# Second MLP product by seven half-size products in three of four quarters, weight sums on GpSimd, low parts by accumulating DMAs

## The reference, cut to what matters

```python
def squared_relu_mlp(h, w1, w2):
    return jnp.square(jax.nn.relu(h @ w1)) @ w2
...
        x = x + squared_relu_mlp(rms_norm(x, norm_mlp[i]), mlp_w1[i], mlp_w2[i])
```

## Time and profile before

| | |
|---|---|
| median of 3 runs | 2765.72 us (2764.86 to 2770.12) |
| the profiled execution: its time, its span | 2773.47 us, 2771.7 us |
| mean granted TensorE clock | 0.993 |
| busy share: TensorE, ScalarE, VectorE, GpSimd | 98%, 39%, 38%, 49% |
| matmuls of the MLP (L2009) | 6,144 |

### The profile page before, as it was taken

How to read it: one execution, slowest core, us unless ns; L and a number is a source line. 1 busy time by engine, 2 the same in 40 slices (tenths; PEclk the granted TensorE clock), 3 DMA queues, 4 the chain that set the end, 5 groups by cost and what they waited for, 6 DMA issues and landing times.

```text
span 2771.7 us, 37296 instructions
## 1 busy us (share of the span) xinstructions
PE 2716.1 (98%) x14594; PEld 2193.4 (79%) x14594; DVE 1046.8 (38%) x1966; ACT 1086.8 (39%) x1649; POOL 1359.7 (49%) x1042
## 2 busy tenths in 40 slices
PE   8999999999999999999899999999999999999999
PEld 6977688888766788888788887888888977688887
DVE  4044622113486512213777874311123044622112
ACT  5355633223446423324334344322234355533222
POOL 4577354445455354445444442445455576345443
PEclk9999999999999999999899999999999999999999
DMA  4322122323422123223312110232323322122232
GB/s 143 99 69 63 52 92 91 106 91 92 106 46 77 61 92 106 91 91 110 80 33 57 37 62 24 92 98 91 106 91 99 100 54 69 56 97 91 92 105 76
DMA packets 273439, 227.87 MB, mean 82 GB/s; under 512 B 29220, under 2 KB 260388, under 8 KB 273300
## 3 DMA queue, kind: packets, MB, share of 16 engines
q1 hardware_dynamic: 262578, 216.66, 25.9%
q10 hardware_dynamic: 10722, 9.28, 1.5%
HBM read 223.62 MB, written 2.30 MB: 82 GB/s over the span
## 4 chain that ended last, share of the span: by engine, by line
PE 91%; DVE 3%; ACT 2%; POOL 2%; issue 1%; DMA 1%; ACTq 0%; SPq 0%; DVEq 0%; POOLq 0%
PE bank L2009 50%; PE bank L1916 20%; PE bank L2132 4%; PE bank L2372 2%; PE bank L2512 2%; PE bank L2092 1%; PE bank L2189 1%; PE bank L2205 1%; POOL w_lo L620 1%; PE bank L1962 1%; PE bank L2169 1%; PE bank L2162 1%; PE bank L2219 1%; POOL arena L693 1%; PE bank L1943 1%
## 5 line engine op out<-in xcount | busy, mean ns | idle before, releaser
L620 POOL TENSOR_TENSOR w_lo<-raw,w_hi 128x512 fp32r<-128x512 f32 x808 | 1081.0, 1368 | 1087.0 <-ACT w_hi L777 1067.7
L777 ACT ACTIVATE w_hi<-raw 128x2048 fp32r<-128x2048 f32 x201 | 383.7, 1909 | 462.1 <-PE bank L2009 423.3
L2009 PE MATMUL bank<-h_hi,w_hi 128*128 128x512 f32 x1024 | 400.8, 391 | 0.0
L2009 PE MATMUL bank<-g_hi,w_hi 128*128 128x512 f32 x1024 | 398.6, 389 | 0.0
L2009 PE MATMUL bank<-h_hi,w_lo 128*128 128x512 f32 x1024 | 398.4, 389 | 0.0
L2009 PE MATMUL bank<-g_hi,w_lo 128*128 128x512 f32 x1024 | 398.4, 389 | 0.0
L2009 PE MATMUL bank<-h_lo,w_hi 128*128 128x512 f32 x1024 | 398.4, 389 | 0.0
L2009 PE MATMUL bank<-g_lo,w_hi 128*128 128x512 f32 x1024 | 398.4, 389 | 0.0
L1916 PE MATMUL bank<-h_hi,w_hi 128*128 128x512 f32 x776 | 317.3, 409 | 2.4 <-POOL w_lo L620 1.9
L1916 PE MATMUL bank<-h_lo,w_hi 128*128 128x512 f32 x776 | 310.5, 400 | 0.0
L1916 PE MATMUL bank<-h_hi,w_lo 128*128 128x512 f32 x776 | 307.8, 397 | 0.0
(11 more groups left out here) (276 smaller groups left out, 3805.0 us busy)
## 6 DMA issues: line engine op xcount, KB each, us to landing
raw<-in_mlp_w SPq DMA_DIRECT2D x128, 1024.0 KB, 5.4
raw<-in_a_w_in SPq DMA_DIRECT2D x48, 512.0 KB, 5.1
raw<-in_c_w_in SPq DMA_DIRECT2D x32, 512.0 KB, 5.5
raw<-in_a_w_in SPq DMA_DIRECT2D x12, 1024.0 KB, 5.2
raw<-in_b_w_in SPq DMA_DIRECT2D x18, 256.0 KB, 4.0
raw<-in_a_w_out SPq DMA_DIRECT2D x4, 1024.0 KB, 4.9
raw<-in_b_w_in SPq DMA_DIRECT2D x4, 1024.0 KB, 5.4
arena<-bias_scratch ACTq DMA_DIRECT2D x16, 256.0 KB, 3.6
```

The costliest lines, as they stand in the source:

```text
L620: ins = nc.gpsimd.tensor_tensor(w_lo[s][:, k, :], raw[s][:, k, :], w_hi[s][:, k, :].bitcast(F32), ALU.subtract)
L777: nc.scalar.activation(w_hi[s][:], raw[s][:], ACT.Copy).then_inc(w_hi_done, 1)
L2009: mm = nc.tensor.matmul(lin_bank[j][:], w[s][:, c, P * j:P * j + P], a[:, c, :], start=c + z == 0, stop=c == CT - 1 and z == 2)
```

## The change

In quarters 0 to 2 of each layer (`HALVED`) the second product of a chunk is made by a seven-product scheme (`down`): contraction tiles are taken in even and odd pairs, the chunk's two output tiles as two column tiles, the 512 tokens as two halves of 256. Of the chunk's weights three of four blocks are used as they are (`weight`), and four sums of blocks are formed (`weight_sum`); of the hidden activations four blocks and three sums (`hidden`, `hidden_sum`). Seven products of 4 contraction pairs x 3 matmuls of 256 columns go to parts of four PSUM banks, and VectorE adds them to or subtracts them from `x` in eight pieces of 128 x 256 (`add_part`). The fourth quarter keeps its form.

The weight sums are formed on GpSimd (`summed_weights`, four instructions of 128 x 512). Low parts of whole chunks and of the sums are formed otherwise than before: ScalarE writes the high part, then its negative into the low buffer, and a DMA issued by GpSimd adds the raw values to it (`add_raw`, and `add_sums` for the sums, which is written in the same way), two DMAs of 512 KB a chunk. The low parts of the three blocks used as they are come from VectorE (`weights_low`, 128 x 512). The sums of activations are formed by VectorE (`differences`, 128 x 256), rounded by ScalarE (128 x 768) and their low parts formed by VectorE. The loops over the quarters are written out on all engines. The diff, cut:

```diff
...
+        w_sum = [part(4 * TOK).rearrange("p (k q n) -> p k q n", k=4, q=4) for _ in range(2)]
...
+        ws_hi = [over_arena(f"ws_hi{s}", [P, 4, 4, P]) for s in range(2)]
+        ws_lo = [over_arena(f"ws_lo{s}", [P, 4, 4, P]) for s in range(2)]
+        gt_hi, gt_lo = over_arena("gt_hi", [P, 4, 3, HALF]), over_arena("gt_lo", [P, 4, 3, HALF])
...
+        def quads(m):
+            return m.rearrange("p (q z) (n c) -> p (z n) q c", z=2, n=2)
+        def half_banks(d):
+            return [bank[k][:, 0:HALF] for k in ((2, 3, 4, 5), (6, 7, 0, 1))[d % 2]]
...
+            def add_raw(n):
+                s = n % 2
+                for half in range(2):
+                    k = slice(4 * half, 4 * half + 4)
+                    pool.wait_ge(w_neg, 2 * split_no[n] + half + 1)
+                    pool.dma_start(w_lo[s][:, k, :].bitcast(F32), raw[s][:, k, :],
+                                   accum_op=ALU.add).then_inc(w_added[s][half], 16)
+            def summed_weights(n):
+                s, v = n % 2, 4 * half_no[n]
+                whole, sums = quads(raw[s][:]), w_sum[s]
+                pool.wait_ge(raw_loaded[s], raw_value[n])
...
+                nc.gpsimd.tensor_tensor(sums[:, 0], whole[:, 3], whole[:, 1], ALU.add).then_inc(ws_summed, 1)
+                pool.wait_ge(ws_summed, v + 1)
+                nc.gpsimd.tensor_tensor(sums[:, 1], sums[:, 0], whole[:, 0], ALU.add).then_inc(ws_summed, 1)
+                pool.wait_ge(ws_summed, v + 2)
+                nc.gpsimd.tensor_tensor(sums[:, 2], sums[:, 1], whole[:, 2], ALU.add).then_inc(ws_summed, 1)
+                nc.gpsimd.tensor_tensor(sums[:, 3], whole[:, 0], whole[:, 1], ALU.add).then_inc(ws_summed, 1)
...
+            def rounding(n):
+                if halved(n):
+                    sums_rounded(n)
+                    weights_rounded(n)
+                    return
                 s = n % 2
...
+                act.wait_ge(raw_loaded[s], raw_value[n])
+                if n >= 2:
+                    act.wait_ge(lin_done, tile0[n - 1])
+                if CHUNKS[n][0] != "mlp":
+                    nc.scalar.activation(w_hi[s][:], raw[s][:], ACT.Copy).then_inc(w_hi_done, 1)
+                    return
+                parts = [slice(4 * half, 4 * half + 4) for half in range(2)]
+                for k in parts:
+                    nc.scalar.activation(w_hi[s][:, k, :], raw[s][:, k, :], ACT.Copy).then_inc(w_high, 1)
+                for half, k in enumerate(parts):
+                    act.wait_ge(w_high, 2 * split_no[n] + half + 1)
+                    nc.scalar.activation(w_lo[s][:, k, :], w_hi[s][:, k, :].bitcast(F32), ACT.Copy,
+                                         scale=-1.0).then_inc(w_neg, 1)
+            def sums_rounded(n):
+                s, v = n % 2, half_no[n]
+                act.wait_ge(lin_done, tile0[n - 1])
+                for half in range(2):
+                    k = slice(2 * half, 2 * half + 2)
+                    act.wait_ge(ws_summed, 4 * v + 2 * half + 2)
+                    nc.scalar.activation(ws_hi[s][:, k], w_sum[s][:, k], ACT.Copy).then_inc(w_high, 1)
+                    act.wait_ge(w_high, 2 * split_no[n] + half + 1)
+                    nc.scalar.activation(ws_lo[s][:, k], ws_hi[s][:, k].bitcast(F32), ACT.Copy,
+                                         scale=-1.0).then_inc(w_neg, 1)
+                    if half == 0:
...
+                        nc.scalar.activation(quads(w_hi[s][:])[:, 0], quads(raw[s][:])[:, 0], ACT.Copy).then_inc(wp_high, 1)
+            def weights_rounded(n):
+                s = n % 2
+                nc.scalar.activation(quads(w_hi[s][:])[:, 2:4], quads(raw[s][:])[:, 2:4], ACT.Copy).then_inc(wp_high, 1)
...
+            def squares(li, q, p, z):
...
+                act.wait_ge(relu_done, g + 1)
+                if p or q:
+                    act.wait_ge(gt_done, 4 * u - 2) if z == 0 else act.wait_ge(gl_done, v - 1)
+                dst = pieces[:, 3:5, :] if z else pieces[:, 0:2, :][:, ::-1, :]
+                src = sq[z].rearrange("p (k n) -> p k n", k=2)
+                nc.scalar.activation(dst, src, ACT.Square).then_inc(gsq_done, 1)
+            def even_high(li, q, p):
+                act.wait_ge(gt_done, 4 * pair_no(li, q, p) + 1)
+                nc.scalar.activation(by_half(g_hi[:, 2 * p, :]), pieces[:, 1:3, :], ACT.Copy).then_inc(gh_done, 1)
+            def odd_high(li, q, p):
...
+                nc.scalar.activation(by_half(g_hi[:, 2 * p + 1, :]), pieces[:, 3:5, :], ACT.Copy).then_inc(gh_done, 1)
+                act.wait_ge(gt_done, 4 * pair_no(li, q, p) + 4)
+                nc.scalar.activation(gt_hi[:, p], pieces[:, 5:8, :], ACT.Copy).then_inc(gh_done, 1)
             def mlp(li, i, m):
-                n = first_chunk["mlp", i]
...
+                for q in range(HALVED):
+                    n, _, Q, X = quarter(li, q)
+                    for p in range(4):
+                        squares(li, q, p, 0)
+                        even_high(li, q, p)
+                        if p < 2:
+                            round_ahead(n + p)
+                        if p == 3:
+                            weights_rounded(n + 4)
+                        squares(li, q, p, 1)
+                        odd_high(li, q, p)
+                        if p == 2:
+                            sums_rounded(n + 4)
+                    for k in range(3, 8):
...
+            def weights_low(n, k):
+                s = n % 2
+                whole, high, low_ = (quads(m[s][:])[:, (0, 2, 3)[k]] for m in (raw, w_hi, w_lo))
+                dve.wait_ge(wp_high, 2 * half_no[n] + (1, 2, 2)[k])
+                nc.vector.tensor_tensor(low_, whole, high.bitcast(F32), ALU.subtract).then_inc(wp_low, 1)
+            def relu(li, q, p, z):
+                n, T, Q, X = quarter(li, q)
...
+                dve.wait_ge(lin_done, T + 2 * p + z + 1)
+                if p or q:
+                    dve.wait_ge(gsq_done, g - 1)
+                nc.vector.scalar_tensor_tensor(sq[z], lin_bank[z][:], 0.0, rs, ALU.max, ALU.mult).then_inc(relu_done, 1)
+            def low(dst, src, high, value):
+                dve.wait_ge(gh_done, value)
+                nc.vector.tensor_tensor(dst, src, high.bitcast(F32), ALU.subtract).then_inc(gl_done, 1)
+            def even_tile(li, q, p):
+                relu(li, q, p, 0)
+                dve.wait_ge(gsq_done, 8 * (QUARTERS * li + q) + 2 * p + 1)
+                nc.vector.tensor_tensor(pieces[:, 2, :], pieces[:, 1, :], pieces[:, 0, :], ALU.subtract).then_inc(gt_done, 1)
+                low(by_half(g_lo[:, 2 * p, :]), pieces[:, 1:3, :], by_half(g_hi[:, 2 * p, :]),
+                    parts_before(li, q) + 3 * p + 1)
+            def odd_tile(li, q, p):
+                relu(li, q, p, 1)
+                dve.wait_ge(gsq_done, 8 * (QUARTERS * li + q) + 2 * p + 2)
+                low(by_half(g_lo[:, 2 * p + 1, :]), pieces[:, 3:5, :], by_half(g_hi[:, 2 * p + 1, :]),
+                    parts_before(li, q) + 3 * p + 2)
+            def differences(li, q, p):
...
+                nc.vector.tensor_tensor(pieces[:, 5, :], pieces[:, 4, :], pieces[:, 0, :], ALU.subtract).then_inc(gt_done, 1)
+                dve.wait_ge(gt_done, v + 1)
+                nc.vector.scalar_tensor_tensor(pieces[:, 6, :], pieces[:, 4, :], -1.0, pieces[:, 2, :], ALU.mult,
+                                               ALU.subtract).then_inc(gt_done, 1)
+                dve.wait_ge(gt_done, v + 3)
+                nc.vector.scalar_tensor_tensor(pieces[:, 7, :], pieces[:, 6, :], -1.0, pieces[:, 3, :], ALU.mult,
+                                               ALU.subtract).then_inc(gt_done, 1)
+            def odd_sums(li, q, p):
+                low(gt_lo[:, p], pieces[:, 5:8, :], gt_hi[:, p], parts_before(li, q) + 3 * p + 3)
+            def add_part(d, c, half, k, op, signal):
+                dst = x[:, c, HALF * half:HALF * half + HALF]
+                nc.vector.tensor_tensor(dst, dst, half_banks(d)[k], op).then_inc(signal, 1)
+            def first_parts(li, q, d):
+                u = pair_no(li, q, d)
+                dve.wait_ge(part_done, 6 * u + 1)
+                add_part(d, 2 * d, 0, 0, ALU.add, part_added)
+                dve.wait_ge(part_done, 6 * u + 2)
+                add_part(d, 2 * d + 1, 1, 1, ALU.subtract, part_added)
+            def down(li, q, d):
+                u = pair_no(li, q, d)
+                n = quarter(li, q)[0] + 4 + d
+                if d:
+                    first_parts(li, q, d)
+                dve.wait_ge(part_done, 6 * u + 3)
+                dve.wait_ge(part_added, 6 * u + 1)
+                add_part(d, 2 * d, 0, 2, ALU.add, part_added)
+                dve.wait_ge(part_done, 6 * u + 4)
+                add_part(d, 2 * d, 1, 1, ALU.add, part_added)
+                if d < 3:
+                    weights_low(n + 1, 0)
+                dve.wait_ge(part_done, 6 * u + 5)
+                dve.wait_ge(part_added, 6 * u + 4)
```

(58 more changed lines are left out.)

276 lines of the change are left out of this document (156 added, 120 removed).

## The result

The changed kernel takes 2897.87 us (median of 4 runs, 2888.75 to 2908.03) against 2767.52 us of the kernel before on the same chip: a ratio of 1.0464, 95% interval 1.0443 to 1.0485, so 4.6% slower. Its profiled execution has a span of 2898.0 us (before: 2771.7) and a mean granted clock of 0.975 (0.993).

What follows compares the result with a forecast made beforehand. TensorE's array time was taken to bound the kernel. Saving 3.2 us but waiting 12.8 us in each of 12 quarters gave +115 us, the clock +10: +125 in all, 2891 us forecast, range 2810 to 2975.

Steps and rivals of the forecast that it cites:

- case A: Likeliest outcome: ScalarE and VectorE delay each other, VectorE and GpSimd collide; 2891 us, own range 2850 to 2935, chance 0.55.
- array time: Halved second products: 256-column matmuls at 0.120 us make 43.53 us into 40.32, saving 3.21 us a quarter, 38.5 in all.
- waits: TensorE's waiting in a halved quarter, at tile 6 and in the second product: 12.8 us a quarter.
- Prices: Added instructions: ScalarE 1.06 us for 1,024 elements, GpSimd sums 1.29 us each, DMA issue 0.37 us.
- The accumulating DMAs: Low parts of weights: 4.4 us to land plus 0.37 us of issue on GpSimd's queue.
- hidden, with 2.8 us to spare: A weight chunk's first half lands about 8.1 us after its buffers come free, against a tile pair's 10.88 us.
- my 0.6 there: Wait forecast in the second chunk of the halved second product: 0.6 us a quarter.
- C: Rival: accumulating DMAs are slow, over 7 us for issue and landing, every weight chunk late; about 3000 us, chance 0.18.
- The circle: ScalarE and VectorE in tiles 2 to 6: a turn takes 12.2 us against 10.88, so tile 6 starts 1.1 us late.
- The collisions: GpSimd's sums from 28.0 us stretch VectorE's differences from 0.43 to 1.38 us; tile 6 starts 4.1 us late.
- The entry: Start of the halved second product: waits of 4.0 us for tile 6's low part and 1.9 us at the third product.
- The clock: Half speed after waits: 6.5 us a quarter, a quarter of the lost work counted, 0.8 us a quarter, +10 us.

Runs made afterwards that it cites:

- e12: As e11, with VectorE's order at the entry of the second product repacked and GpSimd's held-back sums started at tile 7's low part: 2756.72 us, ratio 0.9961.
- e7: Changed kernel with every instruction beside TensorE cut to an eighth of its columns in 8 quarters (wrong values): 2789.11 us.
- e1: Changed kernel with no quarter halved; low parts still from ScalarE's negation and accumulating DMAs, loops unrolled: 2775.14 us, ratio 1.0025.
- e2: Changed kernel with w2's loads in the halved quarters cut from 1 MB to 128 KB (wrong values): 2867.96 us.
- e5: Changed kernel with GpSimd's four sums cut to an eighth of their columns in 8 halved quarters (wrong values): 2866.97 us.
- e8: Changed kernel with sums' low parts on VectorE, plain chunks' on GpSimd, no accumulating DMAs, first chunk's sums rounded between steps of tiles 4 and 5: 2830.97 us.
- e9: As e8, with VectorE's next even-tile relu, ScalarE's square of tile 6 and the sum for the seventh product moved earlier: 2819.67 us.
- e11: As e9, with GpSimd's sums for the second chunk held back until VectorE's last differences, and three order changes on VectorE and ScalarE: 2782.15 us.

## Why the prediction was right, and what in it was not

The total was right (2891 forecast, 2898 measured, case A), and so was the mechanism in the main: TensorE waits at tile 6 and at the entry of the second product, for VectorE. That the total came so close is partly luck, for two terms were off by 40 and 46 us in opposite directions. The quarter without waits is 44.05 + 39.88 = 83.9 us (e12's mean first product, with the norm's matmuls in a layer's first quarter, and e7's second). The changed kernel has 98.0: 9.5 of waits and 4.6 more. The kernel before has 87.6. The spans differ by 126.3 us.

| term, 12 quarters | predicted | measured |
|---|---|---|
| array time | −38.5 | −44 (12 x 3.65) |
| waits | +154 (12.8 each) | +114 (9.5 each) |
| clock, and steps under 0.3 us over the usual | +10 | +56 (4.6 each) |
| sum | +125 | +126 |

*Array time.* Right: 0.120 us a step in the earlier trace rows, 0.1187 in e7. The last quarters of the layers, at nothing in the sum, are longer by 0.7, 1.9, 0.9 and 0.0 us.

*Prices.* ScalarE's 1,024 elements took 1.04 to 1.06 us (1.06 said), sums 1.3 to 2.0 (1.29 alone). GpSimd's issue of an accumulating DMA was mis-sized: 0.87 us, not 0.37.

*The accumulating DMAs.* I took 4.8 us, issue included. Where no load ran beside them the sums' DMAs landed after 4.8 us (median of 25 in the changed kernel, 4.5 to 5.2). The plain chunks' took 6.3 in the median; of "hidden, with 2.8 us to spare" the first half still held for them (e1), with some 1.5 us less to spare. But I never asked where the sums' DMAs for the second chunk fall: beside a load, 7.0 to 8.4 us. This wait of 2.9 us, nearly a third of all, was missed; my 0.6 there was for VectorE. It is C's mechanism at one place in four chunks. The Trainium skill's "SBUF — State Buffer" (the "DVE blocks DMA" trap) speaks of VectorE's two-port modes; I let it lean to C, and no run here shows it at work: e2 keeps VectorE's work and loses the wait. By the Trainium skill's "DMA: Bandwidth & Descriptors" (Anatomy of one DMA, SWDGE path) the landing would have been 3.2 us, an estimate; the trace has 4.8.

*The circle.* "One turn of the circle is 12.2 us", and so tile 6 late by 1.1 us without collisions: this step failed. e5 has the same ScalarE work and no wait at tile 6.

*The collisions.* The mechanism was right, and the place (sums at 28.3 us, 28.0 said; 1.5 and 1.4 us for 256 elements, 1.38 said). Its size was not: tile 6 waits 2.0 us in the mean, not 4.1. Where all three differences meet a sum (7 of 12 quarters) it waits 2.4 to 3.6 us, where two do (2 quarters) 1.4, and where one or none does (3 quarters) 0 to 0.9. The Trainium skill says in "SBUF — State Buffer" (SBUF: two separate sides) that a VectorE instruction with two SBUF inputs and a GpSimd instruction that reads SBUF exclude each other for a whole instruction. The trace agrees: 0.42 us alone, 1.4 to 1.5 beside a sum, and a relu out of a bank stays at 0.68.

*The entry.* `g_lo` of tile 6: 4.0 said, 2.9 measured (4.2 to 4.6 in four quarters). Product 3: 1.9 said, 1.3 measured. The first and third low parts, the low sums and product 7: 1.7 said together, 0.2 measured.

*The clock.* This step failed most. "Half speed in tiles 6 and 7 costs nothing, since TensorE would wait 4 us for `g_lo` anyway", and only a quarter of 6.5 us at half speed counted. Measured is 10.2 us a quarter at 0.50, and only 1.1 of it lies inside a wait. In the other 9.1 a step of 256 columns takes 0.213 us and not 0.119, which loses 4.0 us of the 4.6 left over; the rest was not taken apart. In the changed kernel every wait of 2.4 us or more has a stretch at 0.50 that begins in it or less than 2 us behind it, and none of the seven of 1.3 to 1.4 us has one. e5's 8 quarters show the cost by contrast: 1.8 us less waiting than in the changed kernel's 8, 6.8 us less at half speed, 4.5 us shorter.

## What to carry to other kernels

A scheme that trades array time for work on three other engines is paid at the places where the array changes from one product to the next; count the chains that end there and find their order before counting the array's gain. On this kernel 3.65 us a quarter could be had (e7), and came out as a gain of 0.4% only when GpSimd's sums were moved out of VectorE's critical steps, the sums' DMAs were dropped and VectorE's queue was put in the order of need, all together (e8 to e12). Price each wait of some microseconds with the half-speed stretch behind it: in the changed kernel these cost half as much again as the waits (4.6 us on 9.5). That is no fixed price: in e8 three of twelve waits of 3.2 us, and in e9 two of eleven of 2.6, had no such stretch.

## What the runs showed of the hardware

- Two kinds of transfers share the DMA engines visibly. In the changed kernel 512 KB SBUF to SBUF, accumulating, landed in 4.5 to 5.2 us with no load beside it, and the second chunk's in 7.0 to 8.4 us beside a 1 MB load; in e2, with loads of 128 KB, these took 4.5 to 5.2.
- A 256-element VectorE instruction of 0.42 us took 2.25 us beside a GpSimd sum of 1.58: it began 0.4 us ahead of the sum, during the issue of an accumulating DMA, and ended 0.3 us after it. What held it before the sum began was not taken apart.
- In e11 waits of 0.7 and 1.2 us stand in each second product, and the clock is at 1.00 through all 8 later quarters; in e12 a wait of 1.8 us stands there and the clock is at 1.00 through all 12. In the changed kernel it is at 0.50 after waits of about 4 us. At 0.50 a step of 256 columns is 0.213 us, 1.8 times the 0.119.
